# Order of the high and low products in a split-weight matmul: both tiles' low products, then both tiles' high products

## The reference

```python
def squared_relu_mlp(h, w_up, w_down):      # 1024 -> 4096 -> 1024, twice
    u = jax.nn.relu(h @ w_up)
    return (u * u) @ w_down
...
f = (jax.nn.silu(h @ w_gate[i]) * (h @ w_up[i])) @ w_down[i]   # 1024 -> 2816 -> 1024
```

## Time and profile before

| what | value |
|---|---|
| median of 3 runs | 990.01 us (989.69 to 990.48) |
| span of the profiled execution, first to last instruction | 988.3 us |
| instructions | 16726, of them 6679 matmuls |
| TensorE busy with matmuls | 979.1 us, 99% |
| weight loads, beside the matmuls | 897.2 us, 91% |
| VectorE, ScalarE, GpSimd busy | 76%, 55%, 9% |
| DMA | 166.5 MB, mean 168 GB/s |

### The profile page before, as it was taken

The page is one execution under the profiler, slowest core; times in us unless marked ns, Lnnn a source line. Parts: engine busy times, 40 slices in busy tenths (PEclk is TensorE's granted clock), DMA queues, the critical chain, the costliest instruction groups (busy, mean ns, idle before and its releaser), DMA issues.

```text
span 988.3 us, 16726 instructions
## 1 busy us (share of the span) xinstructions
PE 979.1 (99%) x6679; PEld 897.2 (91%) x6679; DVE 748.5 (76%) x1128; ACT 548.2 (55%) x818; POOL 87.9 (9%) x91
## 2 busy tenths in 40 slices
PE   9999999999999999999999999999999999999998
PEld 8999998888888998999988888999999988888898
DVE  6888778977764499767987844479877988776776
ACT  6642266655454375756665544456566665556444
POOL 5334101000201000001000201001001000000000
PEclk9999999999999999999999999999999999999999
DMA  8733444666655836435476565626536367655551
GB/s 253 239 121 93 133 128 150 196 191 195 188 181 189 252 112 206 148 109 164 141 218 188 175 197 187 191 57 185 185 107 207 112 192 212 191 180 176 182 168 43
DMA packets 164716, 166.50 MB, mean 168 GB/s; under 512 B 6784, under 2 KB 162832, under 8 KB 164640
## 3 DMA queue, kind: packets, MB, share of 16 engines
q1 hardware_dynamic: 162752, 163.47, 53.8%
q0 software_dynamic: 1056, 1.19, 0.5%
q10 hardware_dynamic: 832, 0.79, 0.4%
HBM read 163.82 MB, written 1.08 MB: 167 GB/s over the span
## 4 chain that ended last, share of the span: by engine, by line
PE 88%; DVE 8%; issue 2%; ACT 1%; POOL 0%; ACTq 0%; DVEq 0%
PE ps L667 30%; PE ps L666 15%; PE ps L650 4%; PE ps L651 3%; PE ps L652 3%; PE ps L663 3%; PE ps L646 3%; PE ps L644 3%; PE ps L645 3%; DVE w_lo L1943 2%; PE ps L895 2%; PE ps L602 2%; PE ps L610 2%; PE ps L657 2%; PE ps L658 2%
## 5 line engine op out<-in xcount | busy, mean ns | idle before, releaser
L1943 DVE TENSOR_TENSOR w_lo<-w_raw,w_hi 128x1024 fp32r<-128x1024 f32 (+4 forms) x314 | 375.8, 1206 | 130.7 <-ACT w_hi L1381 128.1
L1381 ACT ACTIVATE w_hi<-w_raw 128x1024 fp32r<-128x1024 f32 x298 | 313.3, 1054 | 207.2 <-PE ps L667 88.0
L667 PE MATMUL ps<-xs,w_hi 128*128 128x512 f32 x728 | 257.1, 396 | 0.0
L666 PE MATMUL ps<-xs,w_lo 128*128 128x256 f32 x728 | 203.5, 279 | 0.0
L667 PE MATMUL ps<-us,w_hi 128*128 128x512 f32 x498 | 176.3, 397 | 0.0
L667 PEld LDWEIGHTS ps<-xs,w_hi 128*128 128x128 f32 x728 | 136.7, 188 | 30.3
L666 PE MATMUL ps<-us,w_lo 128*128 128x256 f32 x498 | 139.9, 281 | 0.0
L666 PEld LDWEIGHTS ps<-xs,w_lo 128*128 128x128 f32 x728 | 137.1, 188 | 2.2
L667 PEld LDWEIGHTS ps<-us,w_hi 128*128 128x128 f32 x498 | 93.6, 188 | 22.7
L666 PEld LDWEIGHTS ps<-us,w_lo 128*128 128x128 f32 x498 | 93.5, 188 | 0.4
L650 PE MATMUL ps<-xs,w_hi 128*128 128x256 f32 x320 | 92.6, 289 | 0.0
(11 more groups left out here) (435 smaller groups left out, 1891.1 us busy)
## 6 DMA issues: line engine op xcount, KB each, us to landing
w_raw<-in_mlp_w_up SPq DMA_DIRECT2D x64, 512.0 KB, 4.3
w_raw<-in_mlp_w_down SPq DMA_DIRECT2D x64, 512.0 KB, 3.5
w_raw<-in_a_w_in SPq DMA_DIRECT2D x32, 512.0 KB, 4.5
w_raw<-in_w_gate SPq DMA_DIRECT2D x22, 512.0 KB, 4.4
w_raw<-in_w_up SPq DMA_DIRECT2D x22, 512.0 KB, 4.7
w_raw<-in_w_down SPq DMA_DIRECT2D x20, 512.0 KB, 3.9
w_raw<-in_w_kv SPq DMA_DIRECT2D x16, 512.0 KB, 4.6
w_raw<-in_w_in SPq DMA_DIRECT2D x16, 512.0 KB, 4.1
```

The costliest lines, as they stand in the source:

```text
L666: mm(ps[:, bank, 0:S], lo[:, kk, w], x[:, kt, 0:S], start=False, stop=False)
L667: o = mm(ps[:, bank, :], hi[:, kk, w], x[:, kt, :], start=False, stop=last)
L1381: o = fn(dst, raw, ACT.Copy)
L1943: return v.tensor_tensor(d, x, y, ALU.subtract)
```

## The change: both low products, then both high products

In kind "feat" the two output tiles are no longer done one after the other within a k tile. In the first k tile of a pair both high products come first and then both low products; in every other k tile both low products come first and then both high ones. Number, shapes and operands of the matmuls are the same, as are the semaphores.

```diff
@@ -637,6 +637,17 @@
                 for kk in range(kk0, kk0 + nk):
                     kt = kt0 + kk
                     first, last = kt == 0, kt == last_kt
+                    if kind == "feat":
+                        low = [(ps[:, 2 * pset + n, 0:S], lo[:, kk, n * P:(n + 1) * P]) for n in tiles]
+                        if not first:
+                            for o_ap, w in low:
+                                mm(o_ap, w, x[:, kt, 0:S], start=False, stop=False)
+                        for n in tiles:
+                            o = mm(ps[:, 2 * pset + n, :], hi[:, kk, n * P:(n + 1) * P], x[:, kt, :], start=first, stop=last)
+                        if first:
+                            for o_ap, w in low:
+                                o = mm(o_ap, w, x[:, kt, 0:S], start=False, stop=last)
+                        continue
                     for n in tiles:
                         bank = 2 * pset + n
                         if kind == "direct":
@@ -657,14 +668,6 @@
-                        elif kind == "feat":
-                            w = slice(n * P, (n + 1) * P)
-                            if first:
-                                mm(ps[:, bank, :], hi[:, kk, w], x[:, kt, :], start=True, stop=False)
-                                o = mm(ps[:, bank, 0:S], lo[:, kk, w], x[:, kt, 0:S], start=False, stop=last)
-                            else:
-                                mm(ps[:, bank, 0:S], lo[:, kk, w], x[:, kt, 0:S], start=False, stop=False)
-                                o = mm(ps[:, bank, :], hi[:, kk, w], x[:, kt, :], start=False, stop=last)
```

## The result

| | before | with the change |
|---|---|---|
| median | 990.13 us (989.69 to 990.48, 4 runs) | 983.8 us (983.32 to 984.06, 4 runs) |
| span of the profiled execution | 988.3 us | 982.0 us |

The ratio is 0.9937, with a 95% interval of 0.9925 to 0.9948: the change makes the kernel faster by 6.3 us, or 0.6%. I had forecast no change, with the full price of rival B, 985.1 us, as the lower end, so both the direction and the range missed.

A forecast was written before the change was run, and what follows sets the result against it. TensorE's matmul-start spacing was taken to bound the kernel; every term was 0, so the span stayed 988.3 + 0 = 988.3 us and the median 990.0 us, with a range of 985.1 to 995.0 us.

The forecast's parts named there:

- rival B: Paired products on xs and us: new order speeds up slower pairs, 2.1 us plus 2.8 us, to 985.1 us; chance 0.23.
- What bounds the kernel: Whole kernel: TensorE, busy 99% of the span and hardly waiting, so distances between successive matmul starts make the time.
- a step's length goes by the product that is streaming, not by the one that follows: Paired k tiles: steps from low products stay 0.12 us, from high ones 0.24, whatever follows; 0 change.
- the term of 0: The 674 reordered k tiles: 0.12 + 0.12 + 0.24 + 0.24 us before and the same after, so 0.
- Runs of short products: Low products side by side, each covering a weight load: pure rows at 0.118 to 0.120 us show no overrun; cost 0.
- The ends of quanta and pairs: Last matmul, its semaphore and the waits at quantum and pair ends stay as before: cost 0.
- Rival A: Pairs on xs: low products lose their long neighbour, 8.3 us slower, 998.3 us, half effect 994.2; chance 0.21.

The follow-up runs named there:

- e5: Kernel before, with the new order only in the last k tile of each pair of the down projections (on us): 987.63 us, ratio 0.9976.
- e11: Changed kernel, with the old order in the last k tile of each pair of the down projections (on us): 986.01 us, ratio 0.9958.
- e9: Changed kernel, but on us, from a pair's second quantum on, two k tiles together, four low products then four high: 983.97 us, ratio 0.9938.
- e7: Kernel before (old order), with xs allocated last, at an odd multiple of 64 bytes: 988.65 us, ratio 0.9984.
- e8: Changed kernel with everything in the second half of memory 64 bytes further, so us starts at a multiple of 128 bytes: 988.94 us, ratio 0.9989.
- e10: Changed kernel with weight buffers 64 bytes further and everything from h on 128 bytes further: 984.61 us, ratio 0.9945.
- e6: Changed kernel with xs allocated last of the fixed tensors, at an odd multiple of 64 bytes: 978.19 us, ratio 0.9883.

## Why the prediction was wrong

- **What bounds the kernel** was right. TensorE's spacing sets the time, its listed waits add up to 5.0 us before and 5.3 after, and all of the gain that could be placed is in that spacing.
- **The step that failed** is "a step's length goes by the product that is streaming, not by the one that follows", from which the term of 0 came. It leaves out what stood ahead. The runs showed instead that a low product takes 118 ns behind a high one and 113 behind a low one, and a high product 226 behind a low pair and 236 behind a high one: 693 ns for a k tile on us instead of 707. I took each kind of step from one place, at 0.01 us, and a difference of 5 ns in 118 is half of such a unit; over 1348 pairs of products it is microseconds. Worse, the few new steps that I could see stand in the first k tiles, not in a steady row, and e5 and e11 show that a step depends on its row's history.
- **The sign was in the trace of before.** In down0, just behind the low-to-low step of the first k tiles, it reads:

```profile
280.62 0.28 PE L666 MATMUL ps<-us,w_lo 128*128 128x256 f32 x1
280.73 0.39 PE L667 MATMUL ps<-us,w_hi 128*128 128x512 f32 x1
280.95 0.28 PE L666 MATMUL ps<-us,w_lo 128*128 128x256 f32 x1
281.07 0.40 PE L667 MATMUL ps<-us,w_hi 128*128 128x512 f32 x1
```

  A low product of 0.11 and a high one of 0.22 us, once, and then 0.12 and 0.24 again: exactly the fast half of the new k tile. Taken as the step that each new k tile would repeat, it gives 707 - 113 - 226 - 118 - 236 = 14 ns for each of 258 k tiles on us, 3.6 us, and the right sign.
- **Runs of short products** were rightly priced at 0 as a danger: two loads in a row do no harm, and four (e9) do none either. I read the pure rows of 0.118 as the floor, though, while they were the slow one of two levels. The fast one stood in the trace of before, in the row on xs_b shown under e5 and e11, on one of the tensors that I left out.
- **The ends of quanta and pairs** cost 0, as said.
- **Rival A** (slower on xs) did not come: 3272 products on xs take 490.5 against 490.7 us.
- **Rival B** had the right idea, that the order can break what slows the products, and the wrong place. It put 2.1 us on xs and 2.8 on us; measured are 0.1 on xs, where the two pair lengths of 5.56 and 5.64 us became one of 5.59, and 5.5 on us, 2.3 of them on direct products that the change does not touch. No rival had an effect beyond the moved instructions. That is what took the time below the range.

## What to carry to other kernels

Where TensorE is the bound and hardly waits, the spacing of matmul starts in whole nanoseconds is the profile to read, stage by stage and as a pattern over several instructions, and an edit that only reorders them can be worth half a per cent. Try equal products side by side (it paid on us and brought nothing on xs as placed here), look at what a row of short products inherits from the product ahead of it, and try the streamed tensor 64 bytes further on against the weight buffers. Order, placement and the split of the long product together gave 1.9% here, and e7 shows that placement alone gave a small part of it.

## What the runs showed of the hardware that was not expected

- A row of products of 256 columns in this 4-byte type runs at one of three steady levels at the full clock (1.000): 113, 118 or 120 ns. 113 and 118 occur for the same instructions on the same addresses, depending on what ran ahead (e5, e11), and in one row on xs_b with the same instructions just ahead.
- The levels go with the start of the streamed tensor against the weight buffers. With the two a multiple of 128 bytes apart, as xs is in the kernel before and us in e8 and e10, a row takes 120 ns; with 64 bytes more between them, 118 or 113 (xs in e6, e7 and e10, us in the other kernels). Only these two relations were tried.
- Why there are levels at all, and what carries the memory from one product to the next, stays open. No run here looks inside a matmul.
